# Gate rows in a tile of their own, short products moved, and the first tile's sum on TensorE, in a two-layer diffusion step

## The reference, cut to what matters

```python
for l in range(DEPTH):
    ...
    xp = xp + mp[2] * out_p
    xs = xs + ms[2] * out_s
    hp = modulate(rms_norm(xp, g_ffn[l]), mp[3], mp[4])
    hs = modulate(rms_norm(xs, g_ffn[l]), ms[3], ms[4])
    xp = xp + mp[5] * grouped_moe(hp, w_router, b_router, w_gate[l], w_up[l], w_down[l])
    xs = xs + ms[5] * grouped_moe(hs, w_router, b_router, w_gate[l], w_up[l], w_down[l])
y_prompt = rms_norm(xp, g_final)
y_sample = rms_norm(xs, g_final)
```

## Time and profile before

| | us |
|---|---|
| median of three runs | 1059.4 (1057.77 to 1061.82) |
| the profiled execution, its own time | 1060.16 |
| its span in the profile | 1058.4 |
| PE busy | 951.9 (90%) |
| DVE busy | 357.8 (34%) |
| ACT busy | 210.7 (20%) |
| POOL busy | 56.1 (5%) |
| DMA moved | 326.41 MB, mean 308 GB/s |

### The profile page before, as it was taken

The page is one execution under the profiler, slowest core; times in us unless marked ns, Lnnn a source line. Parts: engine busy times, 40 slices in busy tenths (PEclk is TensorE's granted clock), DMA queues, the critical chain, the costliest instruction groups (busy, mean ns, idle before and its releaser), DMA issues.

```text
span 1058.4 us, 14229 instructions
## 1 busy us (share of the span) xinstructions
PE 951.9 (90%) x5480; PEld 458.4 (43%) x5480; DVE 357.8 (34%) x910; ACT 210.7 (20%) x555; POOL 56.1 (5%) x83
## 2 busy tenths in 40 slices
PE   4998999897899898998899999989968998989983
PEld 3445788453333333333444446664533333333321
DVE  2118544346421121112502205783474221211124
ACT  2322543022000000001410005671120000000011
POOL 0000011000000000012000000001000000000120
PEclk9999999998999999999999999999989999999996
DMA  9964499519699999999843325394297999999991
GB/s 379 421 257 194 206 373 419 196 55 391 255 422 420 421 420 420 421 404 402 331 197 110 129 79 200 150 406 163 90 358 292 420 421 421 421 420 419 405 366 59
DMA packets 50020, 326.41 MB, mean 308 GB/s; under 512 B 6732, under 2 KB 7244, under 8 KB 20492
## 3 DMA queue, kind: packets, MB, share of 16 engines
q1 hardware_dynamic: 34400, 281.30, 65.6%
q0 software_dynamic: 10416, 35.56, 8.6%
q10 hardware_dynamic: 5120, 8.39, 2.1%
HBM read 307.34 MB, written 17.99 MB: 307 GB/s over the span
## 4 chain that ended last, share of the span: by engine, by line
PE 68%; DMA 16%; DVE 9%; issue 2%; ACT 2%; SPq 2%; POOL 0%; DVEq 0%; ACTq 0%; POOLq 0%
PE PS L641 23%; PE PS L904 15%; PE PS L954 8%; DMA ring<-in_w_up_dram 6%; DMA work<-in_w_up_dram 6%; PE PS L575 4%; PE PS L729 3%; PE PS L696 2%; DMA ring<-y_scratch,rti 2%; PE PS L607 2%; PE PS L711 2%; PE PS L837 1%; SPq L346 1%; DVE nm L1174 1%; PE PS L866 1%
## 5 line engine op out<-in xcount | busy, mean ns | idle before, releaser
L641 PE MATMUL PS<-ring,work 128*128 128x512 f32 x576 | 254.8, 600 | 1.7 <-ACT work L1831 1.6
L641 PEld LDWEIGHTS PS<-ring,work 128*128 128x128 f32 x576 | 109.3, 192 | 134.0 <-issue 130.8
L904 PE MATMUL PS<-ring,gate_bc 128*64 128x512 f32 x704 | 158.0, 600 | 5.6 <-DVE gate_bc L1525 2.5
L1511 DVE TENSOR_TENSOR gate_bc<-gate_bc,PS 128x256 f32<-128x256 f32 x36 | 15.2, 421 | 274.6 <-ACT gate_bc L1874 274.6
L904 PEld LDWEIGHTS PS<-ring,gate_bc 128*64 128x64 f32 x704 | 50.9, 138 | 98.2 <-issue 93.1
L954 PE MATMUL PS<-ring,work 128*64 128x512 f32 x384 | 87.3, 596 | 3.5 <-DVE work L1516 2.3
L1874 ACT ACTIVATE gate_bc<-PS 128x256 f32<-128x256 f32 x36 | 13.8, 383 | 316.1 <-PE PS L904 316.1
L904 PE MATMUL PS<-work,gate_bc 128*64 128x512 f32 x320 | 72.5, 606 | 0.0
L954 PEld LDWEIGHTS PS<-ring,work 128*64 128x64 f32 x384 | 27.5, 137 | 52.0 <-issue 51.0
L575 PE MATMUL PS<-ring,cs 128*32 128x128 f32 x1536 | 47.0, 274 | 2.6 <-ACT modsb L1725 2.6
L1782 ACT ACTIVATE work<-PS,nm 128x384 f32<-128x384 f32 (+1 forms) x96 | 48.2, 509 | 3.3 <-DVE nm L1174 2.9
(11 more groups left out here) (268 smaller groups left out, 893.2 us busy)
## 6 DMA issues: line engine op xcount, KB each, us to landing
ring<-in_w_mod_dram SPq DMA_DIRECT2D x24, 2048.0 KB, 12.0
ring<-in_w_gate_dram SPq DMA_DIRECT2D x44, 1024.0 KB, 22.2
ring<-in_w_up_dram SPq DMA_DIRECT2D x44, 1024.0 KB, 23.8
ring<-in_w_down_dram SPq DMA_DIRECT2D x44, 1024.0 KB, 19.3
work<-in_w_gate_dram SPq DMA_DIRECT2D x20, 1024.0 KB, 21.1
work<-in_w_up_dram SPq DMA_DIRECT2D x20, 1024.0 KB, 23.3
work<-in_w_down_dram SPq DMA_DIRECT2D x20, 1024.0 KB, 22.6
ring<-in_w_qkv_b_dram SPq DMA_DIRECT2D x6, 2048.0 KB, 13.9
```

The lines of the kernel that those rows point to most:

```text
L641: mm = pe.matmul(PS[:, 2 * t, :], lhs[:, k, P * t:P * (t + 1)], ring[:, s, 512 * k:512 * (k + 1)], start=(k == 0), stop=(k == KC - 1))
L904: mm = pe.matmul(PS[64 * g:64 * g + 64, 4 * b + 1, :], xTx[:, k, :] if b else xTp[:, k, CAP * (e % 2):CAP * (e % 2 + 1)], w[:, 0:2, 512 * ...
L1511: dve.tensor_tensor(hE[:, b, :], sg[:, b, :], PS[:, 4 * b + 1, 256:512], ALU.mult).then_inc(tile_sem(f"h_{tag(b)}", l), 1)
```

## The change

Memory: the kernel is built with `dynamic_dma_scratch_size=8192` in place of the default, which leaves room for a tile `gate_ffn` of its own (8 KB per partition). With it:

- POOL loads `gate_ffn` right behind the first gather of a layer's experts (pair 1). The four loads of `gate_join` go; VectorE copies it out of `gate_ffn` after `rows` (four copies of 64x512, behind a wait for `ld_gate_ffn`). `wq` moves out of the place that `gate_join` takes. `gfin` is loaded behind the last gathers.
- TensorE: `index_pair(1)` and `pick_one(1)` stand between the two halves of `gate_up` of expert 0, `turn_one(1)` behind it, `turn_pair(1)` ahead of `down` of expert 0. `carry` stands around `turn_h` of experts 14 and 15, `join(0)` after the last `down`.
- Tile 0: VectorE adds x to the weighted rows (in `yk`), TensorE adds them in PSUM by `add_rows(l, 0)`, and the norm, its square and the copy back to x read PSUM as for the other tiles (`x_kept` is three, tile 0 is the first of the last norms).
- `sum_shifts` stands two products later, `ffn_cols` ahead of the scale rows, `router_bias` behind the first tile's add.

```diff
-                if l == 1:
-                    pool.wait_ge(*at("gu_main", 1, E - 2))
-                    pool.dma_start(gfin, bc(t_["g_final"])).then_inc(S("ld_gate_ffn"), 16)
+                    if pair == 1:
+                        for vec in range(2):
+                            row_bc(gate_ffn[:, vec, :], l, vec, 5, "ld_gate_ffn")
                 pool.wait_ge(*at("gu_main", l, E - 2))
                 pool.wait_ge(*at("down_main", l, E - 2))
-                for vec in range(2):
-                    for g in range(2):
-                        col = 5 * D + 512 * g
-                        pool.dma_start(gate_join[CAP * g:CAP * (g + 1), vec, :],
-                                       mod_d[l, vec, col:col + 512].partition_broadcast(CAP)).then_inc(S("ld_gate_join"), 16)
-                for vec in range(2):
-                    row_bc(gate_ffn[vec], l, vec, 5, "ld_gate_ffn")
...
+                if l == 1:
+                    pool.dma_start(gfin, bc(t_["g_final"])).then_inc(S("ld_gfin"), 16)
...
-                    if (j, t, k) == (1, 0, 4):
+                    if (j, t, k) == (1, 0, 6):
                         sum_shifts(l)
...
-                    if e == E - 1:
-                        carry(2)
-                        carry(1)
-                    gate_up(0, e, e + 1, (lambda: join(0)) if e == E - 1 else None)
+                    gate_up(0, e, e + 1, next_rows if e == 0 else None)
...
+                join(0)
+                add_rows(l, 0)
+                join(1)
...
                     if j == 1:
+                        ffn_cols(l)
                         dve.wait_ge(*at("ld_rows", l, 80))
...
-                        ffn_cols(l)
-                        router_bias(l)
...
+                            if t == 0:
+                                router_bias(l)
                             norm_ffn(l, t)
...
+                dve.wait_ge(*at("rows_ready", l, 1))
+                dve.wait_ge(*at("ld_gate_ffn", l, 32))
+                for vec in range(2):
+                    for g in range(2):
+                        side = slice(CAP * g, CAP * (g + 1))
+                        ins = dve.tensor_copy(gate_join[side, vec, :], gate_ffn[side, vec, 512 * g:512 * (g + 1)])
+                link(ins)
...
-                    link(last)
-                    link(dve.tensor_tensor(x[:, 0, :], x[:, 0, :], yk[0][:, 0, :], ALU.add))
+                    last = dve.tensor_tensor(yk[0][:, 0, :], yk[0][:, 0, :], x[:, 0, :], ALU.add)
+                last.then_inc(S("r_ready"), 1)
...
-    nc = _bacc.Bacc("TRN2", target_bir_lowering=False, num_devices=1)
+    nc = _bacc.Bacc("TRN2", target_bir_lowering=False, num_devices=1, dynamic_dma_scratch_size=8192)
```

More of the change, by code:

```diff
@@ L247, in hybrid_step_kernel @@
         yk = [ring[:, 4 + k, 0:3072].rearrange("p (t n) -> p t n", t=NT) for k in range(2)]
-        gate_ffn = [ring[:, 4 + vec, 3072:4096] for vec in range(2)]
         wT = [xTx.rearrange("p k n -> p (k n)")[:, 0:NT * P], modsb[:].rearrange("p a b -> p (a b)")[:, D:D + NT * P]]
@@ L613, in first_projection, with carry @@
                             mod_slot(0, 3)
-            def carry(t):
-                for g in range(2):
+            def carry(t, sides=(0, 1)):
+                for g in sides:
                     pe.matmul(PS[:, JOIN[t] + g, :], ident, x[:, t, 512 * g:512 * (g + 1)], start=True, stop=False)
             def add_rows(l, t):
-                pe.wait_ge(*at("r_ready", l, t))
+                pe.wait_ge(*at("r_ready", l, t + 1))
                 for g in range(2):
-                    mm = pe.matmul(PS[:, JOIN[t] + g, :], ident, yk[0][:, t, 512 * g:512 * (g + 1)], start=False,
-                                   stop=l == 0 or t == 2)
-                if l == 0 or t == 2:
+                    mm = pe.matmul(PS[:, JOIN[t] + g, :], ident, yk[0][:, t, 512 * g:512 * (g + 1)], start=False, stop=t > 0)
+                if t:
                     mm.then_inc(S("joined"), 1)
@@ L959, in down, with next_rows @@
                     mm.then_inc(tile_sem(f"down_{tag(b)}", l), 1)
+                def next_rows():
+                    index_pair(1)
+                    pick_one(1)
                 pick_one(0)
@@ L982, in experts @@
                         index_pair(e // 2 + 1)
[L983 to L986 removed]
+                    gate_up(0, e, e + 1, next_rows if e == 0 else None)
                     if e == 0:
[L988 removed]
                         if l == 0:
                             turn_cols(1, 3)
[L991 removed]
+                        turn_one(1)
                     if e == E - 2:
                         turn_w()
[L994 removed]
+                    if e % 2 and e < E - 1:
                         turn_pair((e + 1) // 2)
@@ L997, in experts @@
                         down(0, e - 1, e)
-                    if e == 1:
-                        turn_pair(1)
+                    if e == E - 1:
+                        carry(1, (0,))
                     turn_h(0, e + 1, 2 if e < E - 1 else 0)
-                    if e == 0:
-                        turn_one(1)
+                    if e == E - 2:
+                        carry(2)
+                    if e == E - 1:
+                        carry(1, (1,))
                     if e >= E - 3:
                         down(0, e, e + 1, 3 if e < E - 1 else 1)
+                join(0)
+                add_rows(l, 0)
+                join(1)
                 if l == 1:
                     add_rows(1, 1)
-                join(1)
-                if l == 1:
                     add_rows(1, 2)
@@ L1665, in _ @@
             keep_gated(0, 1)
-            add_first(0)
             weighted(0, 1)
@@ L1686, in _ @@
             weighted(1, 0)
+            keep_gated(1, 1)
             weighted(1, 1)
-            keep_gated(1, 1)
             weighted(1, 2)
-            add_first(1)
-            last_norm(1)
-            last_norm(0)
-            last_norm(2)
+            for t in range(NT):
+                last_norm(t)
         @block.scalar
@@ L1953, in _ @@
                 if l == 0:
-                    act.wait_ge(*at("x_moe", 0, 1))
-                    square("attn", k_[:, 0, :], 0)
-                    hT_odd(1, (0,))
-                    for t in range(1, NT):
-                        act.wait_ge(*at("joined", 0, t))
+                    for t in range(NT):
+                        act.wait_ge(*at("joined", 0, t + 1))
                         square("attn", k_[:, t, :], t, summed(t))
@@ L1965, in _ @@
                 else:
-                    for n, t in enumerate((1, 0, 2)):
-                        act.wait_ge(*(at("joined", 1, t) if t else at("x_moe", 1, 1)))
-                        square("attn", yk[1][:, t, :], t, summed(t) if t else None)
+                    for t in range(NT):
+                        act.wait_ge(*at("joined", 1, t + 1))
+                        square("attn", yk[1][:, t, :], t, summed(t))
 _INS = ['x_prompt', 'x_sample', 'cache_k_a', 'cache_v_a', 'cache_k_b', 'cache_v_b', 'c', 'c_ctx', 'w_mod', 'b_mod',
```

61 lines of the change are left out of this document (25 added, 36 removed).

## The result

The changed kernel takes 1034.5 us (median of four, 1032.55 to 1036.82) against 1060.6 of the kernel before in the same comparison: a ratio of 0.9757, 95% interval 0.9737 to 0.9777. Measured once more beside two experiments it took 1035.7 (0.9764, 0.9749 to 0.978). 1036 was forecast, within 1030 to 1048.

What follows compares the result with a forecast made beforehand. The stream of weights was taken to end each layer's experts, with serial work behind. Gains 7.2 + 1.0 + 9.9 + 6.2 = 24.3 us off 1060.2 give 1035.9, said as 1036, range 1030 to 1048.

Steps and rivals of the forecast that it cites:

- What bounds the kernel: Experts of both layers: TensorE is busy nearly all the time, but a layer's experts end when their stream of weights lets them.
- Sum of the shifts: Ahead of `x_turn`: TensorE's wait for VectorE and slow products behind it go; gain 3.6 us per layer, 7.2 in all.
- Start of the experts: First gathered pair: TensorE's 1.27 us wait goes, `turn_pair(1)` costs 1.0; net gain 1.0 us in layer 0, nothing in layer 1.
- the stream absorbs it: Start of the experts: the `gate_join` copies' delay of the second gather costs nothing; without that cover, 2.8 us per layer.
- End of layer 0: From the last expert to the next projection: 4.6 us by the end of `gate_up`, 1.6 behind it, together 6.2 gained.
- So weights still decide: Layer 1, last `gate_up`: last half of the up matrix lands at 1015.0, TensorE would be there at 1013.9; 6.5 us gained.
- End of layer 1: Last expert to last norm: 6.5 us by 2.7 MB less ahead, 3.4 behind `gate_up`, together 9.9 gained.
- Scratch: POOL's gathers: halving the scratch costs nothing, as they are issued 1.26 us apart while none has landed.
- Half clock in the sums: Rival, ends of the layers: sums still run at clock 0.50, each end about 3 us longer; 1042 us, chance 0.12.
- Late gather: Rival, layer 0: a gather of 13.8 us holds `turn_pair(1)`, so `down` of expert 0 starts at 282; 1041 us, chance 0.12.
- Smaller scratch: Rival, layer ends: half the scratch holds only one gather, so each waits for the one before; near 1100 us, chance 0.05.
- Equal shares: Rival, layer ends: earlier gathers take half the DMA rate, last weights 2.3 us later per layer; 1041 us, chance 0.14.

## Why the prediction was right, point by point

**What bounds the kernel**: right. Inside the experts the stream of weights decides: where `down` of expert 0 starts 2 us earlier, `turn_h` 13 of layer 0 comes 2 us earlier, and the experiment with the late copies moved a wait from a gather to a weight matrix and the time stayed.

**Sum of the shifts**: 7.2 forecast, 4.0 + 4.0 measured in the two layers of both profiles, and 5.2 to 6.4 by undoing it. The half that was argued as "products that then run slowly" is real but comes and goes: four of the six places with the old order have it.

**Start of the experts**: 1.0 forecast, about 1.6 shown, all of it in layer 0. Two steps inside were wrong. That the copies "delay the second gather less than TensorE is ahead by then" is false: it was waited for, 1.85 and 1.83 us. That "the stream absorbs it" is borne out by the late copies. And `turn_pair(1)` ahead of `down` of expert 0, priced at 1.0 us, costs about 2 in layer 0 with its wait for the gather; taking it back gives those up to `turn_h` 13 (240.7 us).

**End of layer 0**: 6.2 forecast, 6.8 and 5.6 measured, but split otherwise. "So weights still decide" was said of layer 1 and carried over to layer 0, with a landing at 485.7 against TensorE at 484.3. The last half of the up matrix was issued at 450.6 and took

```profile
ring<-in_w_up_dram SPq DMA_DIRECT2D x1, 1024.0 KB, 28.2
```

so it landed at 478.8 (with the 4.1 us that the changed kernel is ahead there, 482.9 on the scale of before), 1.2 us ahead of TensorE's second half (480.0). TensorE's own order set that end before (the half landed at 489.3, TensorE came to it at 490.2), and sets it now; in the second profile, where TensorE waits 0.50 us, the two nearly meet. Behind it, 17.2 us were forecast and 18.2 and 18.8 measured; TensorE still waits 1.53 us for the norm of tile 0.

**End of layer 1**: 6.5 + 3.4 forecast, 7.6 + 3.0 measured. The forecast let TensorE wait 1.1 us for the weights. It waits 0.17 in the first profile, and in the second the half lands 2.0 us before TensorE comes to it, with a stretch of 25.4: here too "weights still decide" did not hold, and the gain is 1.1 and 1.5 us larger than forecast. Neither half of the change would have done it: with the order alone undone the stretch is 31.6 us, with the loads alone 28.4, with both (before) 33.3, against 25.8. The later of the two counts, so their prices don't add. The 3.0 behind it were right in size, and no one part brings them. Before, TensorE waited 3.75 us ahead of its first sum and then ran it at low pace. With `join(0)` back and tile 0 on TensorE it waits 1.23 us, with tile 0 back and `join(0)` behind the last `down` 0.86, at full pace in both: either edit alone does it, and the other then adds nothing here. VectorE's weighting begins 3.0 us behind the end of `gate_up` 15 in all three, so the loads have no part in it.

**Scratch**: the step of the prediction that failed. "Halving it costs nothing" was given no lower bound, and it gains 3 us, in POOL's DRAIN behind the last store, a stretch that the prediction did not look at although the span of before showed it: the last norm ends at 1048.4, the span at 1058.4, and a store takes 3.2 of those 10 us. In the first profile this gain happens to stand against what the low clock at 700 us took. Without the one the span would have gained 21.7 us, without the other 28.2, and 24.3 were forecast: that is luck.

**Rivals.** Half clock in the sums: no, 1.00. Late gather: a wait of 1.23 us, not 5. Smaller scratch: no, the gathers stand 1.24 us apart.

Equal shares: no, and the trace shows why. These are the queue of the weights (q1) and that of POOL's gathers (q0), with packets, MB and share of the 16 DMA engines, in 7.5 us of before (from 481.8) and in 3.7 us of the changed kernel (from 478.8), while both have work:

```profile
q1 hardware_dynamic: 287, 2.09, 67.0%
q0 software_dynamic: 288, 1.05, 35.0%
...
q1 hardware_dynamic: 136, 1.07, 68.9%
q0 software_dynamic: 136, 0.49, 33.3%
```

The two move equal numbers of packets, and the data packets are 8192 bytes for the weights (a few are 16384 after) and 4096 for the gathers. So two thirds for the weights, 0.28 of 0.42, is what turns packet by packet give, and the prediction misread the row when it said that the trace does not agree with such turns. Its share for the weights was right all the same.

## What to carry to other kernels

Where two chains end at nearly the same point, undo each part of an edit by itself: the parts' prices are not additive, and a part may be worth nothing beside another (here tile 0) or something that nobody meant (here the scratch). Read the whole span, the stretch behind the last useful instruction too. And count a wait of TensorE with the products behind it, but as a range: here 2.0 us of wait cost 2.3 to 4.0.

## What the runs showed of the hardware that was not expected

The stretch between the landing of the last store and the end of the span shrinks with the dynamic DMAs' scratch: 6.8 us at the default, 3.2 to 3.9 at 8192 in all kernels measured, 1.3 at 2048 in both. POOL's DRAIN fills it.

The granted clock can fall without a change in the code: at the end of layer 1's attention it was 0.56 in one profile of the changed kernel and 1.00 in the next, 2.9 us apart. TensorE's waits up to there are the same in both (1.19, 1.25 and 0.76 us in the last 9 us); the clock fell at 699.3, between the 1.25 and the end of the 0.76. Five of the eleven profiles with this code have the fall, for 6.8 us each.

Ahead of the first `x_turn` the code of all kernels is the same but for the sum of the shifts, and yet, with the change to that sum in place, they reach it up to 4.3 us apart (213.9 to 218.2 us). Most of it is the granted clock near 24 us: 0.50 for 6.8 us in the one that is last, for 3.4 us in the six at 216.4 to 217.2, and at full speed in the three at 213.9 to 215.8. In the first profile after (215.8) 1.5 us are two gaps of TensorE of 0.7 us each that wait for nothing the profile shows. Of single terms of 1 to 2 us a single profile therefore tells little.
